# Plain query products, in-place routing and an earlier train of block products in a decoder layer kernel

## The reference, cut to what matters

```python
q  = (hf @ w_q).reshape(T, 8, 2, 128)                  # T = 256 tokens, 8 heads
sc = einsum('thpc,pkc->thpk', q, sub_keys)             # two scores lists of 128 keys a head
v1, i1 = top_k(sc, 16)                                 # best 16 keys of each list
cand = v1[..., 0, :, None] + v1[..., 1, None, :]       # pair sums
top, pos = top_k(cand, 16)                             # 16 experts a head and token
gates = softmax(top)
a = gelu(einsum('cd,ced->ce', x, u[experts]))          # row of u for every expert picked
y = einsum('ce,ced->cd', gates * a, v[experts])        # and row of v
```

## Time and profile before

| | us |
|---|---|
| median of 3 runs | 956.62 (954.1 to 958.07) |
| the profiled execution | 956.16 |
| its span, first to last instruction | 954.3 |
| first indirect DMA issued | 292.4 |
| first dot | 306.1 |

### The profile page before, as it was taken

One profiled execution on the slowest core, in us unless ns is written; L12 is line 12 of the kernel. 1 busy time (PEld: TensorE's weight loads), 2 busy tenths in 40 slices (PEclk: granted clock), 3 DMA queues, 4 the chain that ended last, 5 costly groups with the idle time before them and its releaser, 6 DMA issues.

```text
span 954.3 us, 15802 instructions
## 1 busy us (share of the span) xinstructions
PE 852.9 (89%) x5888; PEld 550.4 (58%) x5888; DVE 665.3 (70%) x1558; ACT 415.1 (43%) x998; POOL 376.3 (39%) x307
## 2 busy tenths in 40 slices
PE   8999999999988787867857999979886799999997
PEld 7999997799977443424413666644342455333333
DVE  5424685564568988987868778769997877344465
ACT  5534565544664663555334344433433224212252
POOL 1000074050005555766443434424447556444351
PEclk9999999999999997988887999988589778999999
DMA  8888523266328899999999999988899999999995
GB/s 308 240 197 237 180 101 121 89 259 242 147 107 303 332 406 395 368 417 412 380 400 402 403 401 398 410 322 316 306 341 364 415 395 356 415 411 416 408 366 222
DMA packets 55027, 303.19 MB, mean 318 GB/s; under 512 B 11515, under 2 KB 14959, under 8 KB 21777
## 3 DMA queue, kind: packets, MB, share of 16 engines
q0 software_dynamic: 37152, 225.29, 59.9%
q1 hardware_dynamic: 14968, 74.03, 21.2%
q10 hardware_dynamic: 2832, 2.88, 2.1%
HBM read 343.80 MB, written 1.54 MB: 362 GB/s over the span
## 4 chain that ended last, share of the span: by engine, by line
PE 60%; DVE 14%; DMA 12%; ACT 6%; issue 5%; POOL 3%; POOLq 0%; SPq 0%; DVEq 0%; ACTq 0%
PE y L1127 14%; PE ps L1168 8%; PE ps L759 7%; PE ps L760 6%; PE ps L761 6%; PE y L1200 6%; DMA late_ring<-in_experts,arena 5%; DMA arena<-in_experts,arena 5%; DVE late_ring L2090 5%; PE ps L1187 3%; POOL arena L2301 2%; DVE w_lo L1668 2%; DMA late_ring<-in_experts,expert 2%; ACT w_hi L1280 2%; PE y L1086 1%
## 5 line engine op out<-in xcount | busy, mean ns | idle before, releaser
L2301 POOL DMA_INDIRECT arena<-in_experts,arena x168 | 216.0, 1286 | 252.7 <-PE ps L1130 210.0
L2090 DVE CUSTOM_DVE_ANT_0 late_ring<-arena 128x1024 f32<-128x1024 f32 x182 | 221.5, 1222 | 93.6 <-DMA arena<-in_experts,arena 89.5
L1127 PE MATMUL y<-arena,diag 64*64 64x512 f32 x808 | 229.6, 698 | 58.0 <-ACT diag L1514 57.8
L1127 PEld LDWEIGHTS y<-arena,diag 64*64 64x64 f32 x808 | 55.6, 150 | 187.7 <-ACT diag L1514 94.4
L1130 PE MATMUL ps<-arena,diag 64*64 64x512 f32 x576 | 162.5, 691 | 0.0
L1500 ACT ACTIVATE acts<-dots 128x2 f32<-128x2 f32 x124 | 25.2, 203 | 310.2 <-DVE dots L2090 310.0
L1668 DVE TENSOR_TENSOR w_lo<-raw,w_hi 128x2048 fp32r<-128x2048 f32 x38 | 89.5, 2356 | 72.8 <-ACT w_hi L1280 72.8
L1130 PE MATMUL ps<-late_ring,diag 64*64 64x512 f32 x376 | 111.5, 723 | 0.0
L759 PE MATMUL ps<-h_hi,w_hi 128*128 128x256 f32 x384 | 110.4, 288 | 0.0
L760 PE MATMUL ps<-h_lo,w_hi 128*128 128x256 f32 x384 | 108.9, 284 | 0.0
L761 PE MATMUL ps<-h_hi,w_lo 128*128 128x256 f32 x384 | 108.8, 283 | 0.0
(11 more groups left out here) (335 smaller groups left out, 1655.3 us busy)
## 6 DMA issues: line engine op xcount, KB each, us to landing
raw<-in_panels SPq DMA_DIRECT2D x40, 1024.0 KB, 5.1
arena<-in_panels SPq DMA_DIRECT2D x6, 1024.0 KB, 6.9
late_ring<-in_up SPq DMA_DIRECT2D x12, 512.0 KB, 8.6
late_ring<-in_experts SPq DMA_DIRECT2D x12, 512.0 KB, 7.9
x<-in_up SPq DMA_DIRECT2D x8, 512.0 KB, 8.3
x<-in_experts SPq DMA_DIRECT2D x8, 512.0 KB, 8.5
arena<-in_experts,arena POOLq DMA_INDIRECT x168, 13.8
arena<-line_scratch ACTq DMA_DIRECT2D x8, 320.0 KB, 8.5
```

The lines of the kernel that those rows point to most:

```text
L1127: straight = pe.matmul(y[rows, t, cols], diag[rows, a % DIAGS, rows], slot(a)[rows, down], start=False, stop=False, skip_group_check=True)
L2090: i = nc.vector.tensor_tensor_reduce(row if n < len(FIRST_BUFFERS) else products[s % GROUP], row, h_rows[:, u // PEER_HEADS, :], 1.0, 0.0, ...
L2301: nc.gpsimd.indirect_dma_start(out=slot(n), out_offset=None, in_=experts, in_offset=bass.IndirectOffsetOnAxis(ap=expert_rows(u)[:, s:s + 1 ...
```

## The change

- Heads 3 to 7 use a product of plain float32, 16 products of 128x128 by 128x256, with whole panels and the normalised `rowsT` (`whole_query`). Their splits on ScalarE and VectorE are gone. The tokens are turned behind groups 7 and 9, not 40 and 41. The queries stand behind groups 11, 16, 21, 26 and 33.
- The ring: buffers 14 and 15 join at slots 20 and 22, buffer 6 at 46 (was 52), 7 at 60 (was 68), 1 at 74 (was 78). GpSimd waits at slots 46, 60 and 74 for the products of heads 5, 6 and 7 (it waited for their splits). Five buffers are given back from slot 62 on. Slot n then reuses the buffer of n-12 for 23 to 45, of n-13 to n-14 for 47 to 67, of n-9 for 71 to 73, and of n-10 from 75 on.
- Routing reads the scores in place (15 steps). For units 7 to 15 the conversions and the negation go to ScalarE, between VectorE steps that are spread over 14 slots; a unit still begins every 9 slots from slot 80.
- Up products stand behind groups 37 to 56. The first eight gate pieces stand at slots 114, 120, ... 156. `COUNT_AT` is 84 and `LISTS_AT` 100 and 170.

```diff
-SPLIT_LO_AT = {15: 3, 27: 4, 39: 5, 52: 6, 66: 7}
-SPLIT_HI_BEHIND = {4: 3, 11: 4, 17: 5, 23: 6, 30: 7}
-QUERY_BEHIND = {8: 3, 14: 4, 20: 5, 27: 6, 34: 7}
+QUERY_BEHIND = {11: 3, 16: 4, 21: 5, 26: 6, 33: 7}
-TURN_BEHIND = {40: 0, 41: 1}
-UP_FROM = 44
+TURN_BEHIND = {7: 0, 9: 1}
+UP_FROM = 37
-JOINS = {52: 6, 68: 7, 78: 1}
-GIVEN_BACK, GIVEN_FROM = (10, 11, 12), 70
+JOINS = {20: 14, 22: 15, 46: 6, 60: 7, 74: 1}
+GIVEN_BACK, GIVEN_FROM = (10, 11, 12, 14, 15), 62
-    begun = 128 + 4 * q if q < TOKEN_CHUNKS // 2 else 172 + 3 * (q - TOKEN_CHUNKS // 2)
+    begun = 114 + 6 * q if q < TOKEN_CHUNKS // 2 else 172 + 3 * (q - TOKEN_CHUNKS // 2)
+LATE_STEPS = {1: 0, 2: 1, 3: 2, 4: 3, 6: 6, 7: 7, 8: 7, 9: 8, 10: 8, 12: 11, 13: 12, 14: 13}
...
+            def whole_query(h):
...
+                b = begin(name)
+                all_taken("row_turn1_1")
+                for blk in range(2):
+                    for k in range(CHUNKS):
+                        at = k * S + blk * P
+                        mm = pe.matmul(b[:, blk * S:(blk + 1) * S], w[:, at:at + P], rowsT[:, k, :],
+                                       start=(k == 0), stop=(k == CHUNKS - 1))
+                mm.then_inc(product_ready, 1)
...
+            def cast_ranks(u):
+                act.wait_ge(route_step, ranked_count(u))
+                nc.scalar.activation(ranked[:, 1, 0, :], ranked_i[:, 0, :], ACT.Copy, scale=float(PEER_KEYS))
+                nc.scalar.copy(ranked[:, 1, 1, :], ranked_i[:, 1, :]).then_inc(ranks_cast, 1)
+            def cast_top(u):
+                act.wait_ge(top_ready, u + 1)
+                nc.scalar.copy(top_atf[:], top_at[:]).then_inc(top_cast, 1)
+                nc.scalar.activation(neg_top[:], top[:, 0:1], ACT.Copy, scale=-1.0).then_inc(top_negated, 1)
+            def cast_rows(u):
+                act.wait_ge(pick_step, picked_count(u))
+                nc.scalar.copy(expert_rows(u), expert_lists(u, u + 1)).then_inc(experts_ready, 1)
...
-                    nc.vector.tensor_copy(key_cur[:].rearrange("p a b -> p (a b)"),
-                                          scores[:, u * 2 * PEER_KEYS:(u + 1) * 2 * PEER_KEYS]
...
-                    early = [name for name in LOADED_EARLY if LOADED_EARLY[name] == JOINS[n]][0]
-                    pool.wait_ge(w_lo_ready, PANELS.index(early) + 1)
+                    over = [name for name in LOADED_EARLY if LOADED_EARLY[name] == JOINS[n]]
+                    pool.wait_ge(product_ready, PLACE[over[0] if over else "qpeer2_1"] + 1)
```

More of the change, by code:

```diff
@@ L80 @@
 TO_WHOLE = 1.5 * 2 ** 23
+ROUTE_STEPS = 15
+WAITING_STEPS = (2, 3, 4, 7, 8, 9, 10, 13, 14)
+RANK_STEPS_EARLY, RANK_STEPS_LATE = 9, 8
+PICK_STEPS_EARLY, PICK_STEPS_LATE = 4, 3
 def over_slots(unit, first, last):
     n = last - first + 1
-    return {first + i: [(unit, k) for k in range(16 * i // n, 16 * (i + 1) // n)] for i in range(n)}
+    return {first + i: [(unit, k + 1) for k in range(ROUTE_STEPS * i // n, ROUTE_STEPS * (i + 1) // n)]
+            for i in range(n)}
 EARLY_ROUTED = 6
 LATE_ROUTE, ROUTE_SLOTS = 80, 9
+LATE_STEPS = {1: 0, 2: 1, 3: 2, 4: 3, 6: 6, 7: 7, 8: 7, 9: 8, 10: 8, 12: 11, 13: 12, 14: 13}
@@ L97 @@
+SOFTMAX_BEHIND = {3: 2, 8: 3, 18: 4, 24: 5, 31: 6, 38: 7}
+RANKS_BEHIND, TOP_BEHIND, ROWS_BEHIND = {}, {}, {}
 for unit in range(EARLY_ROUTED + 1, UNITS):
     begun = LATE_ROUTE + ROUTE_SLOTS * (unit - EARLY_ROUTED - 1)
[L99 to L102, removed]
-TURN_BEHIND = {40: 0, 41: 1}
-TAKE_TURN_BEHIND = {41: 0, 42: 1}
@@ L107 @@
-UP_FROM = 44
+    for step, at in LATE_STEPS.items():
+        ROUTE_AT.setdefault(begun + at, []).append((unit, step))
+    RANKS_BEHIND[(begun + 3) // GROUP] = unit
+    TOP_BEHIND[(begun + 8) // GROUP] = unit
+    ROWS_BEHIND[(begun + 13) // GROUP] = unit
+    GATES_AT[begun + 14] = unit
+LAST_ROWS_AT = LATE_ROUTE + ROUTE_SLOTS * (UNITS - EARLY_ROUTED - 1) + 6
+TURN_BEHIND = {7: 0, 9: 1}
+TAKE_TURN_BEHIND = {8: 0, 10: 1}
+UP_FROM = 37
 UP_BEHIND = {UP_FROM + b: b for b in range(BLOCKS)}
 TAKE_UP_BEHIND = {UP_FROM + 2 * j + 2: j for j in range(BLOCKS // 2)}
-LISTS_BEHIND = {51: 0, 84: 1}
@@ L111 @@
-LISTS_AT = {106: 0, 171: 1}
-COUNT_AT = 112
+LISTS_BEHIND = {48: 0, 83: 1}
+LISTS_AT = {100: 0, 170: 1}
+COUNT_AT = 84
 ONEHOT_AT = {}
@@ L293, in product_order @@
     query(2, 1)
-    for h in range(QUERIES_FIRST, PEER_HEADS):
-        add(f"qpeer{h}", "act")
-        add(f"key_score{h}", "act")
     for i in range(GROUPS):
+        if i in QUERY_BEHIND:
+            add(f"qpeer{QUERY_BEHIND[i]}", "act")
+        if i - 2 in QUERY_BEHIND:
+            add(f"key_score{QUERY_BEHIND[i - 2]}", "act")
         if i in TURN_BEHIND:
@@ L1541, in take_scores @@
                 b = take(f"key_score{h}")
[L1542 to L1545, removed]
+                took(nc.scalar.copy(by_unit[:, :, h, :], b.rearrange("p (t k) -> p t k", t=TILES)))
             take_query_tile(0, 0)
@@ L1886, in _, with rank_step, choice_step @@
             rows_rstd(0)
-            STEPS = 14
-            def after_step(u, k):
-                dve.wait_ge(route_step, u * STEPS + (k - STEPS))
+            def rank_step(u, done):
+                dve.wait_ge(route_step, ranked_count(u) - 4 + done)
+            def choice_step(u, left):
+                dve.wait_ge(pick_step, picked_count(u) - left)
             def route_step_of(u, k):
-                if k == 0:
+                late = u > EARLY_ROUTED
+                keys = by_lists[:, u, :].rearrange("p (a k) -> p a k", a=2)
+                if k == 1:
                     if u < PEER_HEADS:
@@ L1928, in route_step_of @@
                 elif k == 6:
-                    after_step(u, 6)
+                    if late:
+                        dve.wait_ge(ranks_cast, u - EARLY_ROUTED)
+                    else:
+                        rank_step(u, 5)
                     at = 0
```

111 lines of the change are left out of this document (67 added, 44 removed).

## The result

The changed kernel took 988.97 us (982.47 to 990.67, 4 runs) where the kernel before took 955.95 beside it: a ratio of 1.0332, 95% interval 1.0278 to 1.0386. That is slower by some 32 us by the ratio (33 by the two medians). The forecast was 955.5, range 944 to 967, so it was wrong, and by more than its range. The profiled execution took 990.67 us with a span of 988.9. The distances between marks show where the difference of the spans (34.6 us) lies.

| stage, us | before | predicted | after | difference |
|---|---|---|---|---|
| start to slot 43 | 399.9 | 396.4 | 404.7 | +4.8 |
| slot 43 to 46 | 5.8 | 17.8 | 18.0 | +12.2 |
| 46 to 62 (join at 60) | 35.8 | 36.7 | 44.0 | +8.2 |
| 62 to 73 | 25.9 | 25.9 | 26.0 | +0.1 |
| 73 to last up product | 160.0 | 125 | 135.0 | -25.0 |

What follows compares the result with a forecast made beforehand. DMA at 418 GB/s was taken to bound most of the gather, VectorE the gates. 476.7 + 125 + 121.4 = 723.1 against 725.1, plus 1 us for half clock: 956.2 - 1 = 955.2, stated as 955.5, range 944 to 967.

Steps and rivals of the forecast that it cites:

- the late stage: Last up product to slot 167, VectorE-bound: 121.4 us, built on 97.8 before; new waits on ScalarE would cost nothing.
- the stage of the up products: Slot 73 to the last up product's end: 125 us, first product ending at 18.5, nineteen more at 5.53 each.
- The hole at slot 46: Slot 46's gather waits for head 5's query with two slots in flight: queue empties, 12 us lost, not made up.
- The holes at slots 60 and 74: Gathers waiting for the queries of heads 6 and 7, queue nearly dry at issue: 2 us lost at each.
- The recovered shortfall: Slots 12 to 73: more buffers and plain queries win 3.5 of 5.0 and 1.1 of 1.6 us of lost transfer time.
- The sum by transfers: Slot 73 to last up product: 48.1 MB in 115 us, plus hole of 2 and tail of 8.3: 125.3 us.
- Rival 3: Train of up products doesn't end earlier, being at the DMA limit: 5 us more there, 960 us; chance 0.10.
- Rival 1: Hole at slot 46 only 6 us and late stage 4 us shorter: faster, 946 us; chance 0.30.
- Rival 2: Waits for query products at slots 46, 60 and 74 decide, at low clock: +9, 965 us; chance 0.20.
- The 11.5 us: Slot 73 to 167 becomes shorter by this much, part of 25 us of DMA room; 9.4 spent on one wait.

Runs made afterwards that it cites:

- the second profile of the changed kernel: The changed kernel run again unedited, beside later variants, and profiled once more: 992.66 us, ratio 1.0321 to the kernel before.
- the kernel with both edits: The changed kernel with joins moved to slots 53, 64 and 78 and the first eight gate sums taken eight slots behind their onehots, not six: 953.66 us, ratio 0.9900.
- the mended kernel: The changed kernel with joins at slots 53, 64 and 78 and gate sums nine and seven slots behind their onehots, not six: 946.68 us, ratio 0.9862.

## Why the prediction was wrong

The span of the profile was 36.5 us above the sum of the predicted column. Of these the late stage has 12.9, the stage of the up products 10.0, slots 46 to 62 7.3, and the way to slot 43 8.3 (3.5 of them a gain that was not seen, 4.8 mostly the one execution). The hole at slot 46, on which the prediction spent most of its words, has 0.2.

**The hole at slot 46: right, 12.2 for 12.** Place, cause, chain and size came as said: the issue came 12.6 us behind slot 43 for 12.1, and the dot 5.4 us behind the issue for 5.5.

**The holes at slots 60 and 74: the size was off.** The step that failed is "The queue is nearly dry when the issue comes: 2 us" and "Slot 74 [...] is the same, 2 us". The landings were 7.0 and 6.5 us apart where two slots are 2.2 apart in an unbroken flow, so 4.8 and 4.3 us (2.4 and 4.1 in the second profile of the changed kernel). The chain from the landing of slot 53 (440.3) to the issue took 14.3 us, not 12.1, as the query began at a low clock (0.55 granted from 444 to 446) and took 8.11 us. The six slots in flight took 14.1. That the queue had just run dry doesn't make the hole small: the gather issued then takes its own full time, 6.9 and 5.9 us from issue to dot, and only 2.2 of it are owed anyway. The prediction used this time at slot 46 and forgot it at the other two. The Trainium skill (DMA: Bandwidth & Descriptors, Anatomy of one DMA — SWDGE (gpsimd) path) gives an estimate of 4.0 us for such a transfer. The trace doesn't agree: 5.4, 6.9 and 5.9 us from issue to dot at the three places, each into an empty queue. Four more gathers were issued in that time, but at the 217, 190 and 196 GB/s that the engines moved in it their share is 0.3 to 0.4 MB, at 418 GB/s 1 us or less (an estimate).

**What an empty queue costs beside the gap was left out.** From slot 46 to 59 the changed kernel took 31.8 us for 13 slots, before 29.3. From slot 74 to 80 it took 20.7 us, with joins at 53, 64 and 78 17.8. This is 2.5 and 2.9 us more. The mean of 345 GB/s from 418 to 454 looks like a slow flow, but finer windows of the kernel after show a full one between two ends:

```profile
418.00:426.00 8.00, 0.34 (x4) 0.00 (x0) 1.47 (x5) 0.00 (x0) 6.17 (x7) 0.86 0.85 283
426.00:445.00 19.00, 11.27 (x72) 4.06 (x72) 14.82 (x36) 9.41 (x26) 8.73 (x8) 0.77 1.02 424
445.00:454.00 9.00, 9.00 (x40) 6.89 (x40) 7.25 (x29) 2.93 (x11) 0.00 (x0) 0.86 0.56 233
```

The first end is the start of the flow, 2.6 us short of 418 GB/s. The second, 4.0 us short, is already the next hole: GpSimd had issued its last gather at 435.87 and stood at slot 60, four gathers were left in flight at 445, and the engines' rate fell before the last of them had landed at 454.4. So a waiting issue costs transfer time before the queue is empty, and the prediction counted from the last landing only.

**The recovered shortfall, -4.6 us by slot 73: mostly not there.** Slots 62 to 73 took 26.0 us, before 25.9. With later joins it was between 23.5 and 26.1 in eight profiles, so at most a part of the gain is there, and the profiles don't tell. Up to slot 43 none was seen beyond the spread of the profiles.

**Slot 73 to the last up product: 135.0 for 125.** With later joins, and the train as the change has it, it was 130.4 to 131.0 (132.0 with the conversions on VectorE), so some 4 us are the third hole. The rest in the kernel with both edits: the first product began 14.5 us behind slot 73, 0.9 earlier than the 15.4 predicted, but behind an idle TensorE and at a granted clock of 0.67 (482.4 to 490.5), and ended at 20.9 for 18.5:

```profile
482.37 6.32 PE L1209 MATMUL ps<-rowsT,x 128*128 128x256 f32 x16 [5.52 <-DMA x<-in_up]
```

The nineteen behind it took 109.6 us for 105.1. Most of them came 5.53 us apart as predicted; six between 523 and 561 came 5.9 to 6.8 apart, with the DMA engines at 412 GB/s and waits for diagonals, which fits transfers that set the pace there. The sum by transfers was made at 418 GB/s although the nearest row, of the very stage, had 403: 48.1 MB at 403 are 119.4, with the 8.3 us of the tail 127.7. The windows of the kernel with both edits over the same stage:

```profile
468.00:520.00 52.00, 44.12 (x257) 26.60 (x250) 29.92 (x81) 16.50 (x50) 26.22 (x20) 0.93 0.98 394
520.00:598.00 78.00, 74.29 (x427) 46.71 (x425) 53.27 (x166) 31.64 (x98) 35.52 (x28) 1.00 1.01 406
```

So the step that was mis-sized is "I take 125". Rival 3 (transfers bound the train, 5 us more) named the size, 5.4 to 6.0 us, and its mechanism fits the six slow ones; the first product's low clock, 2.4 us, it did not have. It stands beside, not instead of, the others.

**The late stage: 134.7 us to slot 167 for 121.4.** The sum of VectorE's own work came out: with later sums the stage took 123.3 and 122.9 us to slot 168, where the prediction comes to 123.3. The step that failed is "its results are due two or more slots (5 us) later, so the new waits cost nothing", together with the 97.8 us that it started from, which carry the old waits over unchanged. It looked at waits on ScalarE, which were harmless, and at no wait of VectorE on TensorE except the first onehot's. Up to slot 168 the waits for the sums grew from 3.3 us to 14.5, and to 19.1 in the second profile of the changed kernel; without them (0.8) the stage was 12.9 us shorter, about a us for a us.

Why they grew is not shown. Nothing in the change's diff touches the six slots between onehot and `weigh_acts`, but they last less long: without these waits a slot of the stage takes (136.2 - 14.5)/54 = 2.25 us, before it took (99.7 - 3.3)/40 = 2.41. That is 1 us on six slots, some 8 us on eight sums by this estimate. The spreading over 54 slots is not all of it: with the up products and gates at their old places the waits were still 9.1 us. Views of the kernel before (585 to 727) and of the old places (585 to 732), both up to slot 168:

```profile
DVE late_ring L2174 <- PE ps L1187: 3.3, 3, 1.7
```

```profile
DVE late_ring L2244 <- PE ps L1228: 9.1, 4, 4.4
```

The wait stood in the trace of before, from 467 to the end 14.3 us in eight times, 11.0 of them behind slot 168, and the prediction didn't read it.

**The rivals.** Rival 1 fell. Rival 2, the three product waits decide, was the right one in kind: removing them gave 25 us. It was priced at +9, since it asked for a low clock; the query at slot 46 ran at full clock, and the loss came without it. But it is not the whole: with the joins mended the kernel was still 0.7% slower (1.0035 to 1.0111), and with later sums it was not. By the ratios the 0.033 part like this: 0.026 for the joins; 0.021 for the sums once the joins are mended, of which the kernel before gains 0.010 by the same edit, so 0.011 the change's own; and 0.004 back for the rest of the change. Each of these differences is uncertain by 0.005 or more.

**What the change is worth** without the two faults: 3.4 us, 0.4%, against the kernel before with the same later sums, which the runs can't tell from nothing. The single comparisons give some 0.2% for the earlier train and 0.4% for the moved conversions, both with overlapping intervals. Slot 73 to 168 took 253.4 us in the mended kernel and 254.7 in the kernel before with later sums. The 11.5 us that the prediction expected from these stages weren't there: 5 of them went to the train of up products, and another 5 the kernel before gets by later sums alone (254.7 for 259.7).

## What to carry to other kernels

When a transfer issue is made to wait, count what is in flight against the whole chain up to the issue. If it runs dry even by a little, the price is at once the full time of a transfer into an empty queue less one interval, and the engines already move less while the last few gathers land. Moving the same wait a few slots later took nearly all of the price away. And when work is moved into a stage that one engine binds, list every wait of that engine in that stage, the unchanged ones too: a distance in slots that was enough before is not a distance in time.

## What the runs showed of the hardware

- A gather of 0.887 MB into an empty queue took 5.4 to 6.9 us from issue to dot (slots 46, 60 and 74 of the changed kernel), where in an unbroken flow one lands every 2.2 us.
- The DMA engines of the changed kernel moved 283 GB/s in the 8 us behind an empty queue, 424 in the next 19, and 233 in the 9 us in which the last four gathers in flight landed and none was issued. In the kernel before they moved 418 in the 42 us behind slot 43.
- A plain query of 16 products (32 rows in the trace) took 7.17 us at full clock, as two up products had said, and 8.11 us at slot 60, where it began at a granted clock of 0.55 (444 to 446).
